# First input projection: weight columns loaded in blocks between the row tiles, and its first output tile started on half of the tokens

## What is computed

```python
z = x @ w_in                       # x: 576 x 1024, w_in: 1024 x 2560
q, k, v, xl, gl = jnp.split(z, [512, 1024, 1536, 2048], axis=-1)
...
xc, new_buf = _causal_conv(xl, conv_buf, conv_w, conv_b)
r = jax.nn.sigmoid(... xc @ w_a + b_a)
ig = jax.nn.sigmoid(... xc @ w_x + b_x)
```

## Time and profile before

| | |
|---|---|
| three executions | 728.52, 731.29, 731.52 us; median 731.29 us |
| the profiled execution | 730.15 us, its span 728.5 us (1.65 us lie around the span) |
| TensorE busy | 630.7 us, 87% of the span |
| mean granted TensorE clock | 0.959 of 2.4 GHz |
| transposes of x (L664) | 4.47 to 12.80 us |
| first output tile (L696, L703) | 14.21 to 24.13 us |
| projection without a gap after that | from 24.13 us |

### The profile page before, as it was taken

One profiled execution on the slowest core, in us unless ns is written; L12 is line 12 of the kernel. 1 busy time (PEld: TensorE's weight loads), 2 busy tenths in 40 slices (PEclk: granted clock), 3 DMA queues, 4 the chain that ended last, 5 costly groups with the idle time before them and its releaser, 6 DMA issues.

```text
span 728.5 us, 11355 instructions
## 1 busy us (share of the span) xinstructions
PE 630.7 (87%) x3948; PEld 405.0 (56%) x3948; DVE 267.3 (37%) x566; ACT 159.0 (22%) x322; POOL 111.2 (15%) x191
## 2 busy tenths in 40 slices
PE   6999999999995898979999879899887877777764
PEld 5777676467664565655454636656554444444321
DVE  1562269036456453543544671101110011000257
ACT  2001542143344442431000101111111111111122
POOL 8000000012024133320000002112121111010100
PEclk9999999999998999999999799999999999999987
DMA  9330303153043599972991847999999999999273
GB/s 300 145 113 4 116 0 115 45 184 135 1 141 104 176 363 325 370 278 110 417 385 59 324 187 269 409 416 415 415 419 417 418 418 416 417 415 385 103 287 115
DMA packets 53399, 184.46 MB, mean 253 GB/s; under 512 B 10563, under 2 KB 10563, under 8 KB 44658
## 3 DMA queue, kind: packets, MB, share of 16 engines
q1 hardware_dynamic: 37056, 147.86, 52.1%
q0 software_dynamic: 11328, 29.01, 10.9%
q10 hardware_dynamic: 4978, 7.11, 2.6%
HBM read 174.44 MB, written 18.42 MB: 265 GB/s over the span
## 4 chain that ended last, share of the span: by engine, by line
PE 52%; SPq 20%; DMA 16%; DVE 5%; issue 5%; ACT 3%; POOLq 0%; DVEq 0%; ACTq 0%
PE ps L696 13%; PE ps L930 8%; DMA arena<-in_w_down_e_dram 7%; SPq L384 6%; SPq L387 6%; PE ps L1000 5%; PE ps L745 4%; SPq L383 4%; PE ps L710 4%; DMA arena<-in_cache_k_dram 3%; PE ps L1022 3%; PE ps L816 2%; PE ps L762 2%; DMA arena<-in_w_out_dram 2%; DMA arena<-in_w_in_dram 1%
## 5 line engine op out<-in xcount | busy, mean ns | idle before, releaser
L1000 PE MATMUL ps<-arena 128*64 128x256 f32 x1088 | 124.6, 384 | 14.7 <-DMA arena<-in_w_up_e_dram 13.9
L1000 PEld LDWEIGHTS ps<-arena 128*64 128x64 f32 x1088 | 88.0, 138 | 55.6 <-DMA arena<-in_w_up_e_dram 20.2
L696 PE MATMUL ps<-arena 128*128 128x288 f32 x384 | 95.4, 411 | 1.5 <-DMA arena<-in_w_in_dram 1.4
L1022 PE MATMUL ps<-arena 128*64 128x512 f32 x272 | 68.9, 652 | 25.6 <-DMA arena<-in_w_down_e_dram 15.3
L1722 DVE TENSOR_TENSOR arena<-ps,arena 128x128 f32<-128x128 f32 x34 | 9.9, 292 | 211.7 <-ACT arena L1276 211.7
L696 PEld LDWEIGHTS ps<-arena 128*128 128x128 f32 x384 | 73.7, 193 | 22.5 <-issue 2.0
L1022 PEld LDWEIGHTS ps<-arena 128*64 128x64 f32 x272 | 23.5, 147 | 60.0 <-issue 60.0
L930 PE MATMUL ps<-arena 128*128 128x512 f32 x128 | 56.2, 594 | 0.3 <-DMA arena<-in_w_out_dram 0.3
L816 PE MATMUL ps<-arena 128*128 128x128 f32 x256 | 40.3, 297 | 13.3 <-DVE arena L1502 4.6
L609 POOL DMA_INDIRECT y_rows<-arena x17 | 18.3, 1079 | 180.6 <-ACT arena L1283 153.8
L505 POOL DMA_DIRECT2D arena<-in_cache_v_dram x64 | 34.5, 539 | 69.6 <-PE ps L849 44.4
(11 more groups left out here) (321 smaller groups left out, 768.1 us busy)
## 6 DMA issues: line engine op xcount, KB each, us to landing
arena<-in_w_gate_e_dram SPq DMA_DIRECT2D x34, 1024.0 KB, 17.0
arena<-in_w_up_e_dram SPq DMA_DIRECT2D x34, 1024.0 KB, 24.0
arena<-in_w_down_e_dram SPq DMA_DIRECT2D x34, 1024.0 KB, 24.7
arena<-in_cache_k_dram SPq DMA_DIRECT2D x64, 256.0 KB, 5.4
arena<-in_cache_v_dram POOLq DMA_DIRECT2D x64, 256.0 KB, 6.7
arena<-in_w_in_dram SPq DMA_DIRECT2D x4, 2048.0 KB, 8.5
arena<-in_w_out_dram SPq DMA_DIRECT2D x1, 4096.0 KB, 13.0
x_rows<-arena ACTq DMA_DIRECT2D x8, 512.0 KB, 6.2
```

The lines of the kernel that those rows point to most:

```text
L696: last = mm(ps[:, b + h, 0:HALF], win[n % 2][:, k, m * P:(m + 1) * P], xT[:, k, h * HALF:(h + 1) * HALF], start=k == 0, stop=k == KD - 1)
L1000: last = mm(ps[fh * 64:fh * 64 + 64, u, 0:256], xTm[:, k, u * CAP:(u + 1) * CAP], gu[:, :, k, fh * P:(fh + 1) * P], start=k == 0, stop=k = ...
L1022: last = mm(ps[u * 64:u * 64 + 64, 5 + dh, :], hT[u][:, fh * CAP:(fh + 1) * CAP], dn[u][:, fh, dh * W:(dh + 1) * W], start=fh == 0, stop=f ...
```

## The change

SP's order is new: row tiles 0 to 2 (`FIRST_X = 3`), then columns 0 to 127 of the XL weights for all eight `k` (`s_win0`), then row tiles 3 and 4, then the three other column blocks of XL (`s_win[0]`, 16 each, so 48 in all, and later counts of that semaphore are 32 higher), then Q as before. A block has the same 0.5 MB as a row tile, but its rows in DRAM are 128 numbers (512 bytes) long, where a row of the old load was 512 numbers (2048 bytes).

TensorE transposes row tiles 0 to 2, makes the first output tile for tokens 0 to 287, transposes row tiles 3 and 4, makes the first output tile for tokens 288 to 575, and waits for the three other blocks ahead of the second output tile. The number of transposes, matmuls and copies is the same.

```diff
+FIRST_X = 3
...
-            for t in range(NT - 1):
-                sp.dma_start(x[:, t, :], A["x_prompt"][0, t * P:(t + 1) * P, :]).then_inc(s_x[t], 16)
-            sp.dma_start(x[0:TS, NT - 1, :], A["x_sample"].rearrange("b s d -> (b s) d")).then_inc(s_x[NT - 1], 16)
-            for n, c in enumerate(ORDER):
...
+            def load_w(n, cols, done):
+                src = w_in[:, ORDER[n] * W:(ORDER[n] + 1) * W].rearrange("(k p) n -> p k n", p=P)
+                sp.dma_start(win[n % 2][:, :, cols], src[:, :, cols]).then_inc(done, 16)
+
+            for t in range(FIRST_X):
+                load_x(t)
+            load_w(0, slice(0, P), s_win0)
+            for t in range(FIRST_X, NT):
+                load_x(t)
+            for m in range(1, 4):
+                load_w(0, slice(m * P, (m + 1) * P), s_win[0])
+            for n in range(1, len(ORDER)):
                 if n >= 2:
 
                     sp.wait_ge(s_pj, [4, 8, 20][n - 2])
...
+                load_w(n, slice(0, W), s_win[n % 2])
...
-            for t in range(NT):
+            def x_transpose(t):
                 pe.wait_ge(s_x[t], 16)
...
+            for t in range(FIRST_X):
+                x_transpose(t)
...
-                        for k in range(KD):
-                            if n == 0 and m == 0 and k % (KD // 2) == 0:
-
-                                pe.wait_ge((s_win0, s_win[0])[k // (KD // 2)], 16)
+                        if n == 0 and m == 0:
+
+                            for h in range(2):
+                                if h == 0:
+                                    pe.wait_ge(s_win0, 16)
+                                    for half in range(2):
+                                        pe.wait_ge(s_xe[half], FIRST_X)
+                                else:
+                                    for t in range(FIRST_X, NT):
+                                        x_transpose(t)
+                                    for half in range(2):
+                                        pe.wait_ge(s_xe[half], NT)
+                                for k in range(KD):
+                                    last = mm(ps[:, b + h, 0:HALF], win[0][:, k, 0:P], xT[:, k, h * HALF:(h + 1) * HALF], start=k == 0, stop=k == KD - 1)
+                        if n == 0 and m == 1:
+                            pe.wait_ge(s_win[0], 48)
+                        for k in range(KD if n or m else 0):
                             for h in range(2):
```

More of the change, by code:

```diff
@@ L329, in _, with load_x @@
         def _(sp):
-            for t in range(NT - 1):
-                sp.dma_start(x[:, t, :], A["x_prompt"][0, t * P:(t + 1) * P, :]).then_inc(s_x[t], 16)
-            sp.dma_start(x[0:TS, NT - 1, :], A["x_sample"].rearrange("b s d -> (b s) d")).then_inc(s_x[NT - 1], 16)
-            for n, c in enumerate(ORDER):
+            def load_x(t):
+                if t < NT - 1:
+                    sp.dma_start(x[:, t, :], A["x_prompt"][0, t * P:(t + 1) * P, :]).then_inc(s_x[t], 16)
+                else:
+                    sp.dma_start(x[0:TS, t, :], A["x_sample"].rearrange("b s d -> (b s) d")).then_inc(s_x[t], 16)
+            def load_w(n, cols, done):
[9 more added lines that the diff above has]
+            for n in range(1, len(ORDER)):
                 if n >= 2:
                     sp.wait_ge(s_pj, [4, 8, 20][n - 2])
[L338 to L345, removed]
+                load_w(n, slice(0, W), s_win[n % 2])
             ck = A["cache_k"][0].rearrange("n s h d -> (n s) (h d)")
@@ L655, in _ @@
             pe.wait_ge(s_cst, 1)
-            for t in range(NT):
+            def x_transpose(t):
                 pe.wait_ge(s_x[t], 16)
                 for half in range(2):
-                    n = 2 * t + half
-                    if n >= 2:
+                    if t:
                         pe.wait_ge(s_xe[half], t)
@@ L665, in _ @@
                     last.then_inc(s_xtp, 1)
-            for h in range(2):
-                pe.wait_ge(s_xe[h], NT)
+            for t in range(FIRST_X):
+                x_transpose(t)
             unit = [0]
@@ L686, in _ @@
                 if n:
-                    pe.wait_ge(s_win[n % 2], 16 * (n // 2 + 1))
+                    pe.wait_ge(s_win[n % 2], 16 * (n // 2 + 1) + (0 if n % 2 else 32))
                 if c != V_:
@@ L740, in gate_half @@
                 if c == 0:
-                    pe.wait_ge(s_win[0], 48)
+                    pe.wait_ge(s_win[0], 80)
                 else:
```

## The result

The changed kernel takes 724.96 us (median of 17 executions, 722.61 to 728.83) against 731.21 us before (17 executions beside them, 727.53 to 732.66): **ratio 0.9927, 95% interval 0.991 to 0.9944**, a gain of 4.1 to 6.6 us (the quotient of the two medians, 0.9915, lies inside the interval). The direction and the mechanism were right, the size was not. The profiled execution took 724.43 us.

What follows compares the result with a forecast made beforehand. TensorE bounds the first half, loads the experts at the end; the start waits for XL weights. Terms -1.41, -1.74, +0.77 (copy wait) and +0.53 (row tiles) give -1.85: 730.15 - 1.85 = 728.3 us, range 725.5 to 731.8.

Steps and rivals of the forecast that it cites:

- First half at 11.10 us behind ScalarE's copy: First output tile's first half starts at 11.10 us, released by the copy of row tile 2, and takes 3.90 us.
- the sum: Start of kernel: four terms together -1.85 us, second output tile starting at 22.27 us instead of 24.13.
- 512-byte rows at 27.8 ns: XL column-block loads: each 512-byte packet takes 27.8 ns, interpolated between measured sizes; ends 22.0 and 51.2 ns.
- rival 3: Ahead of the second output tile: last three blocks land late, from 41.8 ns a packet; 732.5 us, chance 0.07.
- The copy covers it at both ends, narrowly at the worse one: First XL block lands at about 9.4 us, 10.9 at worst, before ScalarE's copy lets TensorE start at 11.10.
- Row tiles 3 and 4 cost 3.00 us between the halves: Between first output tile's halves: transposes and copies, uncovered by TensorE, take 3.00 us where 2.47 stood.
- rival 1: Between first output tile's halves: clock falls to 1.2 GHz, costing up to 1.74 us; 730.0 us, chance 0.17.
- The gain reaches the end: Whole kernel: later loads wait on TensorE counts, so all shift by 1.85 us; opposing rival 730.2 us, chance 0.08.
- the wait for weights goes (-1.41), the spell at 1.2 GHz goes (-1.74): Before and in the first output tile: TensorE's 1.41 us weight wait and the slow clock's 1.74 us both disappear.
- the slow stretch from 8 to 10 us: DMA at the start: 223 and 165 GB/s against 393 just before, considered when pricing the first block's landing.
- Rival 4: Later stages: further 1.2 GHz spells, about 1.7 us each, go too; 726.6 us for one, 724.9 for two, chance 0.11.
- SP's issues: SP's queue: a 1024-row load takes 1.2 us to issue; Q's load stands 1.5 us later, hidden until near 46 us.

Runs made afterwards that it cites:

- two runs built on it: Changed kernel with five extra matmuls ahead of the second output tile, ratio 0.9986; changed kernel with GpSimd's gate-block loads issued late, ratio 0.9928.
- all the kernels of the table: Repeats of both kernels and variants of start, loads, TensorE order and gate blocks, against the kernel before; ratios 0.9925 to 1.0081, the highest old loads with new order.
- the fourth trace: The kernel before, profiled again with no edit, against kernels before on the same chip: ratio 1.0006, span 730.1 us.

## Why the prediction was right in kind and wrong in size

- *First half at 11.10 us behind ScalarE's copy.* Right: 10.44, 11.21 and 10.32 us in the three traces, each released by that copy. In the two early ones the 24 transposes ahead of it take 5.23 us, in the other 5.87. Read by durations, as the prediction did, the step to 2.4 GHz comes earlier there: in the first trace four of the last weight loads take 0.42 us, in the second all eight take 1.57, while the clock column reads 1.00 in both. The trace of before that the sum was read from was a late one (from 4.47 to 10.33 us, 5.86); the other three take 5.33, 5.23 and 5.31. This is worth 11.10 - 10.44 = 0.66 us of the first pair's 2.52.
- *512-byte rows at 27.8 ns.* Right from 7 to 7.5 us, low later. In the first trace 322 packets from 7 to 7.5 us at a share of 1.087 are 27.0 ns each, and 858 from 16.5 to 18 us at 1.198 are 33.5 ns:

```profile
q1 hardware_dynamic: 322, 0.16, 108.7%
```

```profile
q1 hardware_dynamic: 858, 0.44, 119.8%
```

  GpSimd's queue had 27 packets in the first window and none in the second, so the higher price is not that of packets from another queue; its cause is open. Both are below 41.8 ns, and no load released the second tile: rival 3 fell. "The copy covers it at both ends, narrowly at the worse one" held in the three traces of the changed kernel, in which the block landed 6.6, 7.4 and 7.3 us after its issue at 2.35, and failed in two runs built on it: there the block came last, at 10.73 and 10.90 us, within the predicted worst case, because the copy had ended earlier than the summed 10.95.
- *Row tiles 3 and 4 cost 3.00 us between the halves.* Measured 17.12 - 14.56 = 2.56. The two halves themselves took 4.12 us each instead of 3.90; the two misses cancel.
- *The clock falls in the new gap* (rival 1): it did not in any of the three traces.
- *The gain reaches the end:* yes. Over all the kernels of the table the ratio follows the start of the second tile: 4.05 us earlier is 0.9945 of 731 us, measured 0.9925 to 0.9947; 7.7 us later is 1.0105, measured 1.0081 (1.0057 to 1.0105).
- *The step that failed* is the first two terms of the sum, "the wait for weights goes (-1.41), the spell at 1.2 GHz goes (-1.74)". The mechanism was right, the size was read from one execution. From the end of the transposes to the weights TensorE waits 1.41, 3.83, 2.97 and 3.25 us in the four traces of before, and the 32 instructions take 9.56, 9.43, 9.68 and 10.91 us. The wait alone is 2.87 us on average, 1.46 more than the sum had, and the 32 instructions take 0.33 more, for the spell of the fourth trace; the transposes end on average where they did in the first trace. Another 0.44 us is the changed kernel, whose second tile starts that much ahead of the sum on average. Together the front gains 4.05 us instead of 1.85. The text named the slow stretch from 8 to 10 us and used it against the new block alone. It did not ask what the old load, which waits at the end of the same queue, would do in an execution in which that stretch is longer.
- *Rival 4* had the size (726.6 and 724.9 us) for a reason that was not shown: nothing behind the second tile differs beyond the scatter. That the range reached as low as it did is owed to this rival, and so to luck.
- *SP's issues:* a load of 1024 rows was taken to hold SP for 1.2 us; block 0 took 0.43 us. In exchange the loads behind the row tiles were held up, and Q landed 3.2 us later than before (ScalarE's first small load, which waits for it, 25.91 against 22.71), not 1.5. Q's slack of 20 us covers both.

## What to carry to other kernels

A load that ends a wait at the start of a kernel is a draw, not a number: take its landing from several executions, and from more than one chip, before pricing the wait, above all when it stands last in a queue that other loads share. An order in which the critical engine waits for an on-chip copy, with the loads due well ahead, gains the mean of that draw and not only the wait of the trace at hand. Reordering loads and reordering the work can each be worth nothing and gain only as a pair, so test both halves alone.

## What was not expected of the hardware

The same load, issued at 3.43 us, landed between 14.07 and 16.51 us in four executions of one kernel, on at least two chips, and the DMA rate from 8 to 12 us was 211 and 265 GB/s even without the gate blocks; what slows that stretch stays open. The clock fell behind a wait of 1.41 us that followed transposes, and stayed at 2.4 GHz behind one of 2.10 us that followed matmuls of 256 columns. A 512-byte packet of SP's queue took 33.5 ns from 16.5 to 18 us, with no other queue at work, and 27.0 from 7 to 7.5.
